# A routed-expert transformer layer in fp32: TensorE runs 52 unread fp32 products of the identity in three of its pauses

## What is computed

```
pg_all = softmax(t @ w_coarse + b_coarse); grp = argmax(pg_all)
fine = (t @ w_fine + b_fine) of that group; top_v, top_i = top_k(fine, 2)
gates = softmax(top_v) * max(pg_all), at the two chosen of 32 experts
a = silu(t @ w_gate[e]) * (t @ w_up[e]) * gates[e]
y = sum over e of a @ w_down[e]
x = x + g2 * y;  out = rmsnorm(x, final_g)
```

## Time and profile before

| what | value |
|---|---|
| time before, median of 3 runs | 1015.23 us (1015.1 to 1015.82) |
| the profiled execution | 1015.25 us, span 1013.4 us |
| mean granted clock of TensorE | 0.955 |
| PE busy | 913.2 us, 90% of the span |
| PE idle ahead of the table, of `turn_x(0)`, of the last stage | 9.1, 7.2 and 10.1 us |

### The profile page before, as it was taken

One profiled execution on the slowest core, in us unless ns is written; L12 is line 12 of the kernel. 1 busy time (PEld: TensorE's weight loads), 2 busy tenths in 40 slices (PEclk: granted clock), 3 DMA queues, 4 the chain that ended last, 5 costly groups with the idle time before them and its releaser, 6 DMA issues. The chain is left out here.

```text
span 1013.4 us, 11938 instructions
## 1 busy us (share of the span) xinstructions
PE 913.2 (90%) x4619; PEld 689.4 (68%) x4619; DVE 517.3 (51%) x649; ACT 413.7 (41%) x572; POOL 129.0 (13%) x103
## 2 busy tenths in 40 slices
PE   2799999999996999888999845999999999999775
PEld 2588889999984555447888724767676767676432
DVE  4753232232325666435656464665656565646048
ACT  4621111111104666503243231766666666656123
POOL 0000000000003910000111002112121212231100
PEclk9899999999996999989999975999999999999978
DMA  9425446311002300011121175799999999997194
GB/s 373 198 109 189 149 182 228 107 42 42 2 1 87 104 1 2 25 46 63 63 83 62 42 302 184 270 366 377 378 354 366 361 369 362 367 362 287 72 379 182
DMA packets 39026, 190.91 MB, mean 188 GB/s; under 512 B 9654, under 2 KB 10806, under 8 KB 23992
## 3 DMA queue, kind: packets, MB, share of 16 engines
q1 hardware_dynamic: 28556, 166.56, 43.6%
q0 software_dynamic: 9216, 18.89, 5.0%
q10 hardware_dynamic: 1200, 4.72, 1.2%
HBM read 178.48 MB, written 26.35 MB: 202 GB/s over the span
## 5 line engine op out<-in xcount | busy, mean ns | idle before, releaser
L1581 DVE TENSOR_TENSOR gu_lo<-w_gu,gu_hi 128x2048 fp32r<-128x2048 f32 x64 | 146.3, 2290 | 115.0 <-ACT gu_hi L1480 114.9
L550 PE MATMUL PS<-h_hi,w_hi 128*128 128x384 f32 x432 | 148.2, 343 | 5.4 <-DVE h_lo L413 5.4
L552 PE MATMUL PS<-h_lo,w_hi 128*128 128x384 f32 x432 | 145.2, 336 | 0.0
L554 PE MATMUL PS<-h_hi,w_lo 128*128 128x384 f32 x432 | 145.1, 336 | 0.0
L1480 ACT ACTIVATE gu_hi<-w_gu 128x2048 fp32r<-128x2048 f32 x64 | 122.0, 1908 | 23.3 <-DMA w_gu<-in_w_gu 23.2
L1767 PE MATMUL PS<-gu_hi,xT_hi 128*128 128x512 f32 x256 | 115.9, 453 | 2.5 <-DVE xT_lo L1587 2.5
L1800 PE MATMUL PS<-w_d,aT 128*128 128x512 f32 x256 | 115.3, 593 | 1.2 <-ACT aT L1500 1.2
L1769 PE MATMUL PS<-gu_hi,xT_lo 128*128 128x512 f32 x256 | 101.8, 398 | 0.0
L1768 PE MATMUL PS<-gu_lo,xT_hi 128*128 128x512 f32 x256 | 101.5, 396 | 0.0
L550 PEld LDWEIGHTS PS<-h_hi,w_hi 128*128 128x128 f32 x432 | 81.7, 189 | 14.2 <-issue 11.0
L552 PEld LDWEIGHTS PS<-h_lo,w_hi 128*128 128x128 f32 x432 | 81.8, 189 | 1.0 <-issue 1.0
(11 more groups left out here) (191 smaller groups left out, 1371.6 us busy)
## 6 DMA issues: line engine op xcount, KB each, us to landing
w_gu<-in_w_gu SPq DMA_DIRECT2D x64, 1024.0 KB, 10.0
w_d<-in_w_down SPq DMA_DIRECT2D x32, 1024.0 KB, 10.2
wm<-in_w_mod SPq DMA_DIRECT2D x10, 2048.0 KB, 8.0
w_raw<-in_w_in SPq DMA_DIRECT2D x18, 512.0 KB, 8.7
yt<-y_rows SPq DMA_DIRECT2D x9, 1024.0 KB, 13.4
xt<-in_x_all SPq DMA_DIRECT2D x9, 512.0 KB, 3.3
h_rows<-h SPq DMA_DIRECT2D x9, 512.0 KB, 2.6
y_all<-yt SPq DMA_DIRECT2D x9, 512.0 KB, 2.7
```

Source lines behind the costliest of these rows:

```text
L550: pe.matmul(o, w_hi[b][:, k, :], h_hi[:, k, tok], start=k == 0, stop=False)
L552: pe.matmul(o, w_hi[b][:, k, :], h_lo[:, k, tok], start=False, stop=False)
L554: last = pe.matmul(o, w_lo[b][:, k, :], h_hi[:, k, tok], start=False, stop=k == KD - 1)
L1581: dve.tensor_tensor(gu_lo[:, n % 3, h, :], w_gu[:, n % 3, h, :], raw(gu_hi[:, n % 2, h, :]), ALU.subtract).then_inc(s_lo, 1)
```

## The change

A helper `keep_busy` issues a number of fp32 products of 512 columns with the identity as the weights. The moving data are the first 128 columns of four planes of `cat`. The output goes to bank 2 of PSUM, and nobody reads it. The products wait for no semaphore and raise none. 18 stand behind the two prefix counts, ahead of the wait for `s_match`. 14 stand behind the table, ahead of the waits of the first `turn_x`. 20 stand behind the overflow section, ahead of the waits of the last stage.

```diff
+                    def keep_busy(count):
+                        for i in range(count):
+                            pe.matmul(PS[:, 2, :], ident[:], cat[:, 0:4, 0:P], start=True, stop=True)
+
                     def table():
...
                     pe.matmul(PS[:, 1, 0:NT * NE], ones[:], flat, start=True, stop=True
                               ).then_inc(s_prefix, 1)
+                    keep_busy(18)
                     pe.wait_ge(s_match, 2)
                     table()
+                    keep_busy(14)
                     pe.wait_ge(s_row7out, 2)
                     pe.wait_ge(s_count, 1)
                     turn_x(0)
...
                     overflow(pe, one_round)
 
+                    keep_busy(20)
                     pe.wait_ge(s_y, NE)
```

## The result

The changed kernel takes 1026.91 us (median of 4 runs, 1025.86 to 1028.07) where the kernel before takes 1015.16 in the same session: a ratio of 1.0116, 95% interval 1.0098 to 1.0134. It is slower by 11.8 us. The prediction was 1025.3 us, so +10.1, and the time lies in its range.

A forecast was written before the change was run, and what follows sets the result against it. PE's path was taken as the bound: waits ahead of table, transposes and last sums, and an unbroken expert stream. Routing +5.6 and last stage +4.5 made +10.1 us, 1025.3 us; the forecast's own range was 1022 to 1028, to 1030 with fallen clock.

The forecast's parts named there:

- The price of a product: Each unread fp32 product of 512 columns on PE: two records of 0.427 us, 0.853 us at full clock, 1.707 at half.
- the gain in the table: Table in the routing: 7.94 us at half clock become about 4.1 at full clock, -3.9 us.
- The slow start: First 18 products: clock rises after 4.7 us, bounds 0 and 6.8, costing half of it, 2.35 us.
- what the clock gives back to `gate_up`: First expert's `gate_up(0, 0)`, 5.25 us before, runs at full clock in some 2.75: -2.6 us with the following transposes.
- the point of 0.66 us a product: All three places: the product price at which the whole change turns sign; part of the faster rival, 4 in 100.
- the 10.4 that the prediction gave for products fully hidden: Faster rival, 4 in 100: products hidden in all three pauses, clock gains of 10.4 us stand alone, 1004.9 us.
- First pause: 18 products ahead of the table: 17.7 us, so the table starts at 619.3 instead of 610.89, 8.4 us late.
- Second pause and transposes: 14 products behind the table take 11.95 us, +4.7 us; then `turn_x(0)` at full clock, -1.0 us.
- The first rival: Clock raised but falls again: in the wait behind `turn_x(0)`, 1027.9 us, or in the table, 1029.7; a quarter.
- Experts: Expert stage, one unbroken PE stream: the routing's sum of +5.6 us all reaches the end of the experts.
- Last stage: 20 products ahead of the last sums: second tile's sum done at 982.8 instead of 978.27, +4.5 us.
- The 0.5 us for the branches: Overflow section's branches ahead of the 20 products, formerly hidden in the pause: 0.5 us, bounds 0 and 2.

The follow-up runs named there:

- second trace of before: The kernel before, unchanged, profiled once more: ratio 0.9997 (0.9987 to 1.0008).
- second trace of the changed kernel: The changed kernel (18, 14 and 20 products), without an edit, profiled once more: ratio 1.0106 (1.0088 to 1.0124) against the kernel before.
- the 14 alone: The changed kernel without the 18 and the 20 products, only the 14 behind the table kept: 1.0038 against before, +3.9 us.
- The two kernels with 6 more products ahead of the prefix counts: Changed kernel with 6 products ahead of the prefix counts, then 10, 8, 11; one also has 2 behind `turn_x(0)`: 0.9918 with the 2, 0.9904 without.
- 8, 8 and 11: The changed kernel with 8, 8 and 11 products in the same three places instead of 18, 14 and 20: 0.9956 against before, -4.5 us.
- 6, 10, 8 and 11: Changed kernel with 6 products added ahead of the prefix counts and 10, 8, 11 in its three places, none behind `turn_x(0)`: 0.9904 against before.

## Why the prediction was right

The price of a product, the overlap with the pauses and the gain in the table were as predicted. The slow start and what the clock gives back to `gate_up` were mis-sized, in opposite directions, so that the time came out 1.6 us from the forecast partly by luck. All numbers count from the first product of the block; where there are two values, they are those of the two traces of the changed kernel against the first of before.

- **The price of a product** was right. The 40 records of the last group lie in 17.17 us, 0.429 each. The Trainium skill, TensorE: Matmul & The Clock Gate, Back-to-back issue gap, has 0.216 us for a product of 512 columns; an fp32 product measured about four times that. With half the columns the change's sign turns, as the point of 0.66 us a product said; the gain was 5.2 us, half of the 10.4 that the prediction gave for products fully hidden.
- **First pause.** Predicted: table 8.4 us late. Measured: 6.8 and 8.0. The clock rose about 1.4 and 3.8 us after the first product, not 4.7: the cost of the slow start was oversized by half a microsecond to 1.6. In the four other traces whose first group stands behind half-clock counts it rose after 1.3 to 1.7 us. The 4.7 leaned on the two rises of one trace, after 5.5 and 5.6 us; in the second trace of before the same two came after 3.2 and 4.0. The bounds of 0 and 6.8 hold all of these. The lines of the second trace of the changed kernel are these.

```profile
600.73 17.52 PE L1806 MATMUL PS<-cat,ident 128*128 128x512 f32 x36
618.09 4.13 PE L1812 MATMUL PS<-entry,match 128*128 128x64 f32 x36
```

- **Table.** Predicted -3.9, measured 3.96 us from start to start in both, where the run with the 14 alone has 7.74 at half clock (611.07 to 618.81), so -3.8: right.
- **Second pause and transposes.** Predicted: 11.95 us for the 14 products; measured 12.08 in both. `gate_up` began 6.8 and 8.0 us late, against 8.2 by the sum.
- **What the clock gives back to `gate_up`** was mis-sized. -2.6 was predicted. `gate_up(0, 0)` took 4.36 us in both traces of the changed kernel, against 5.25 and 4.32 in the two of before, where the clock came back at different points of it: a gain of 0.9 us against the first, and none against the second. Its lines in the second trace of before:

```profile
632.45 0.76 PE L1767 MATMUL PS<-gu_hi,xT_hi 128*128 128x512 f32 x1 [2.46 <-DVE xT_lo L1587]
...
636.77 1.05 PE L1758 MATMUL PS<-ident,xrows 128*128 128x128 f32 x8
```

The first rival, with a quarter of the chance, had a fall of the clock in the wait behind `turn_x(0)`. So it was in the first trace of the changed kernel. In the second the clock came through the wait and fell 1.05 us after `gate_up` had begun at 637.65, as its granted clock shows:

```profile
637.00:638.00 1.00, 0.35 (x2) 0.34 (x3) 0.50 (x1) 1.00 (x1) 0.00 (x0) 1.00 0.41 57
638.00:639.00 1.00, 1.00 (x5) 0.80 (x4) 0.92 (x1) 0.04 (x1) 0.00 (x0) 0.85 0.47 156
```

So the rival's loss came true in most of its size. The time of 1026.9 lies nearer to the rival's 1027.9 than to the forecast's 1025.3, and stays under the rival's since the first pause cost less than the sum had.
- **Experts.** Predicted +5.6 at the last `down`, measured +5.8 and +7.0. At the end of `gate_up(0, 0)` the delay was 5.9 and 7.1 us, so the stage passed it on nearly whole.
- **Last stage.** Predicted +4.5, measured +4.1 against the first trace of before and 4.65 against the second. The 0.5 us for the branches is not there: the products start 3.54 us after the last `down` starts.

The profiled execution of the changed kernel is 12.8 us above that of before. 2.9 of these lie ahead of the block and are scatter, 9.96 in it. The prediction was made against one trace of before, and the scatter ahead of the block, which my range did not name, could have moved a single trace by up to 4 us.

## What to carry to other kernels

Work that keeps a clock up must be shorter than the pause, in microseconds, at the clock at which it starts: here 0.43 us a record at full clock, 0.85 at half. The same three places gave +11.8 us with 44 us of products, and about -5 us with 22 to 23. The two kernels with 6 more products ahead of the prefix counts gave more still, -8.3 and -9.8 us by the ratios, which their intervals don't tell apart. No pause was left open for more than 0.75 us there, except the wait of 2.46 us in one of them, and the clock stayed at 1.00 from 594 us to the last sum. Against half the columns, the block of the first of them is 2.7 us shorter: 1.05 us in the time to the table, where the prefix counts run at full clock, and 1.5 in `gate_up(0, 0)`.

A stage that is cold in one trace may be half warm in the next: read what a clock gives back from two traces of before, not from one.

## What the hardware showed that I had not expected

- In the kernel with 8, 8 and 11 the clock fell while PE was busy with the 64-column fp32 products of the table, 1.62 us of idleness before them (0.61 in the slice 615 to 616). It held through the same table where the gap before it was 0.5 us or none. Whether the gap is the reason was not tested alone.
- Six traces came to the wait of 2.46 us behind `turn_x(0)` at full clock and had nothing in it. In five of them the clock then fell: 0.2 us ahead of the start of `gate_up(0, 0)` in the first trace of the changed kernel, 0.1 us behind it with the 14 alone, 1.0 us behind it in the second trace of the changed kernel and with 256 columns, and 1.5 us behind it with 8, 8 and 11. So it can fall when PE is back at work already. It held in the sixth (6, 10, 8 and 11). In the two traces with 2 products in the wait it held. What decides it stays open; none of the runs moves that wait alone.
- The stages ahead of the change scatter by 4.3 us between traces, though their instructions are the same (589.33 to 593.58). In the two first traces the clock came back at different times in the attention stage, the projection and the last tile; that this is all of the scatter was not tested.
